# Where a ring slot is filled: normalised rows out of slot 7, half a matrix ahead of the ring

## The reference

```python
x = x + merged @ w_out[i]
hn = _rmsnorm(x, ffn_norm_g[i])
# _hier_moe: a group by softmax(hn @ wg), two experts in it by their logits
#   expert e: a = silu(xb @ w_gate[e]) * (xb @ w_up[e]);  y = a @ w_down[e]
x = x + _hier_moe(hn, ...)
return _rmsnorm(x, final_norm_g)
```

## Time and profile before

| | us |
|---|---|
| median of 3 runs (2300.44 to 2302.30) | 2300.65 |
| profiled execution, its own time | 2298.54 |
| its span | 2296.7 |
| TensorE busy | 2176.2 (95%) |
| TensorE weight loads (beside the matmuls) | 1131.4 (49%) |
| VectorE busy | 936.3 (41%) |
| ScalarE busy | 349.3 (15%) |
| GpSimd busy | 297.2 (13%) |
| bytes moved | 563.57 MB, 245 GB/s on average |

### The profile page before, as it was taken

The page is one execution under the profiler, slowest core; times in us unless marked ns, Lnnn a source line. Parts: engine busy times, 40 slices in busy tenths (PEclk is TensorE's granted clock), DMA queues, the critical chain, the costliest instruction groups (busy, mean ns, idle before and its releaser), DMA issues.

```text
span 2296.7 us, 23080 instructions
## 1 busy us (share of the span) xinstructions
PE 2176.2 (95%) x9050; PEld 1131.4 (49%) x9050; DVE 936.3 (41%) x1815; ACT 349.3 (15%) x678; POOL 297.2 (13%) x260
## 2 busy tenths in 40 slices
PE   9999999999999999999999999999999899888886
PEld 6544444475887644477588553333333333333332
DVE  2256544542876587537544342222222222222224
ACT  2015324201222200021101210000000000000001
POOL 0001121221376100001053010000000000000001
PEclk9999999999999999999999999999999999999999
DMA  7211110330333444483332499999999999999997
GB/s 291 101 56 47 55 46 10 115 151 10 110 131 132 160 183 183 172 149 116 128 138 110 201 345 425 427 426 426 426 427 427 426 427 426 426 427 427 427 427 278
DMA packets 75709, 563.57 MB, mean 245 GB/s; under 512 B 21202, under 2 KB 25938, under 8 KB 43152
## 3 DMA queue, kind: packets, MB, share of 16 engines
q1 hardware_dynamic: 52544, 530.70, 57.7%
q10 hardware_dynamic: 15136, 22.71, 3.0%
q0 software_dynamic: 7920, 8.67, 1.1%
HBM read 558.59 MB, written 27.82 MB: 255 GB/s over the span
## 4 chain that ended last, share of the span: by engine, by line
PE 69%; DMA 21%; DVE 6%; SPq 1%; issue 1%; ACT 1%; POOL 0%; DVEq 0%; ACTq 0%; POOLq 0%
DMA sb<-in_eu 13%; PE ps L1193 9%; PE ps L522 9%; PE ps L850 8%; DMA sb<-in_ed 8%; PE ps L429 7%; PE ps L1230 6%; PE ps L771 5%; PE ps L1006 5%; PE ps L454 3%; PE ps L1034 2%; PE ps L732 2%; DVE sb L1704 2%; PE ps L710 2%; PE ps L1164 2%; SPq L3064 1%
## 5 line engine op out<-in xcount | busy, mean ns | idle before, releaser
L1193 PE MATMUL ps<-sb 128*64 128x512 f32 x2048 | 463.0, 607 | 50.9 <-DMA sb<-in_eu 42.4
L1193 PEld LDWEIGHTS ps<-sb 128*64 128x64 f32 x2048 | 163.8, 139 | 337.1 <-issue 337.1
L1704 DVE TENSOR_TENSOR sb<-sb 128x1024 f32<-128x1024 f32 (+9 forms) x419 | 226.4, 573 | 86.3 <-PE ps L850 38.3
L522 PE MATMUL ps<-sb 128*128 128x512 f32 x512 | 236.7, 600 | 0.0
L1230 PE MATMUL ps<-sb 128*64 128x512 f32 x992 | 221.4, 599 | 14.0 <-ACT sb L1672 8.3
L850 PE MATMUL ps<-sb 128*128 128x512 f32 x448 | 193.4, 593 | 1.4 <-DVE sb L2255 1.4
L429 PE MATMUL ps<-sb 128*128 128x512 f32 (+1 forms) x464 | 188.9, 566 | 1.0 <-issue 1.0
L771 PE MATMUL ps<-sb 128*128 128x256 f32 x784 | 175.7, 383 | 3.6 <-DVE sb L2175 3.6
L771 PEld LDWEIGHTS ps<-sb 128*128 128x128 f32 x784 | 148.5, 191 | 25.3 <-DVE sb L2175 4.0
L1230 PEld LDWEIGHTS ps<-sb 128*64 128x64 f32 x992 | 70.6, 137 | 151.9 <-issue 134.9
L522 PEld LDWEIGHTS ps<-sb 128*128 128x128 f32 x512 | 91.0, 190 | 100.3 <-issue 98.6
(11 more groups left out here) (347 smaller groups left out, 2055.5 us busy)
## 6 DMA issues: line engine op xcount, KB each, us to landing
sb<-in_eu SPq DMA_DIRECT2D x63, 2048.0 KB, 36.7
sb<-in_eg SPq DMA_DIRECT2D x62, 2048.0 KB, 37.3
sb<-in_ed SPq DMA_DIRECT2D x60, 2048.0 KB, 37.3
sb<-in_m SPq DMA_DIRECT2D x16, 2048.0 KB, 7.4
sb<-in_m SPq DMA_DIRECT2D x16, 1024.0 KB, 4.9
sb<-in_mg SPq DMA_DIRECT2D x8, 1536.0 KB, 6.5
sb<-in_wo SPq DMA_DIRECT2D x4, 2048.0 KB, 7.7
sb<-in_winF SPq DMA_DIRECT2D x12, 512.0 KB, 3.5
```

Of the source, the lines that this page charges most:

```text
L522: ins = pe.matmul(o, lhsT, rhs, start=k == 0, stop=k == 7)
L1193: ins = pe.matmul(o[64 * e:64 * e + 64, :], x[:, k, 64 * e:64 * e + 64], weight(2 * mat + e)[:, 512 * k:512 * k + 512], start=k == 0, stop ...
L1704: return own(dve.tensor_tensor(o, a, b, op))
```

## The change

- `RING` has place 7 as its seventh entry in place of the tenth: matrix 6 goes there, once the mixer's last products are done; 7, 8 and 9 go to places 3, 1 and 5.
- The normalised rows of blocks 0 to 2 are staged, one after the other, in one buffer of 1024 columns in the constants that are done with, those of block 3 in `YE`. ScalarE waits for the row transfer before it reuses or goes on.
- `first_rows` reads the residual X in its place, with a step of 8 elements, and the one-hots carry the factor `block_r` of the norm.
- Matrix 10: its first half (2048 columns) goes to `FIRST_HALF`, also in the constants, once three row transfers have landed and the ranks and counts are done; the second half goes to its ring slot as before. Users get a column with the matrix, to find the half.
- The count matmuls stand ahead of the last rows of pair 0, `count_rounds` ahead of `weights`.
- The constants are ordered anew and padded by 40 columns.

```diff
-SBUF = 55940
-RING = (6, 2, 0, 4, 8, 9, 3, 1, 5, 7)
+SBUF = 55980
+RING = (6, 2, 0, 4, 8, 9, 7, 3, 1, 5)
+AHEAD = len(RING)
...
+        done_ck = SB[:, 4096 + CK_COLS["c01"][0]:4096 + CK_N + SM_N + 8 * 72 + 72 + 400]
+        at_ck = CK_COLS["neg"][0] - CK_COLS["c01"][0]
+        HELD = [view(done_ck, at_ck, 1024)] * 3 + [YE]
+        FIRST_HALF = view(done_ck, 0, 2048)
...
-                pe.wait_ge(S("hn_rows"), i + 1)
                 pe.wait_ge(S("first"), i + 1)
-                zr = Z[:, i, :].rearrange("p (b a) -> p b a", b=8)
+                zr = X[:, i, :].rearrange("p (a b) -> p b a", b=8)
...
             rank(3)
+            open_tile(pe, ("cnt",), 4)
+            for j in range(4):
+                ins = pe.matmul(T.ap("cnt")[:, 0:64], ck("ones"), ES[:, j, :], start=j == 0, stop=j == 3)
+            ins.then_inc(T.f("cnt"), 1)
             first_rows(2, 1)
...
+            def expert(n, at_):
+                return (FIRST_HALF if n == AHEAD and at_ < 2048 else slot("ex", n))[:, at_:at_ + 512]
...
-                act.activation(Z[:, i, :].rearrange("p (b a) -> p b a", b=8), X[:, i, :].rearrange("p (a b) -> p b a", b=8),
+                if i:
+                    act.wait_ge(S("hn"), 16 * i)
+                act.activation(HELD[i].rearrange("p (b a) -> p b a", b=8), X[:, i, :].rearrange("p (a b) -> p b a", b=8),
                                ACT.Copy, scale=block_r[:, i:i + 1]).then_inc(S("hn_rows"), 1)
                 act.wait_ge(S("hn_rows"), i + 1)
-                act.dma_start(hn_d[128 * i:128 * i + 128, :], Z[:, i, :]).then_inc(S("hn"), 16)
+                act.dma_start(hn_d[128 * i:128 * i + 128, :], HELD[i]).then_inc(S("hn"), 16)
...
                 for c in range(2):
-                    t = tt(OC[:, c, :], AM[:, c, i, :], bc(BM0[:, c, i], 1, 128), ALU.mult)
+                    t = own(dve.scalar_tensor_tensor(OC[:, c, :], AM[:, c, i, :], block_r[:, i:i + 1], bc(BM0[:, c, i], 1, 128),
+                                                     ALU.mult, ALU.mult))
...
             def weights():
+                count_rounds()
...
                     for e in range(2):
+                        if n + e == AHEAD and part < 2:
+                            continue
...
-                if n == 8:
+                if n == 6:
+                    sp.wait_ge(*T.full("mgp", 3, 3, 3))
+                if n == 9:
                     sp.wait_ge(*T.full("wo2", 3, 1))
-                if n == 9:
-                    sp.wait_ge(S("hn"), 64)
-                    sp.wait_ge(*T.full("xt", 0, 1))
+                if n == AHEAD:
+                    sp.wait_ge(S("hn"), 48)
+                    sp.wait_ge(*T.full("rank", 3))
+                    sp.wait_ge(*T.full("cnt"))
+                    for part in range(2):
+                        cols = slice(1024 * part, 1024 * part + 1024)
+                        sp.dma_start(FIRST_HALF[:, cols], EW[k // 2][2 * q + k % 2][:, cols]).then_inc(loaded("ex", n)[0], 16)
```

More of the change, by code:

```diff
@@ L40 @@
 CK_COLS = {}
-CK_N = _cols(CK_COLS, [("ident", 128), ("iota", 128), ("tok", 8), ("gf", 8), ("gx", 8), ("neg", 128), ("cneg", 124), ("c01", 124),
-                       ("tri", 128), ("ones", 128), ("cs", 256)])
+CK_N = _cols(CK_COLS, [("ident", 128), ("iota", 128), ("tok", 8), ("gf", 8), ("gx", 8), ("c01", 124), ("tri", 128), ("ones", 128),
+                       ("neg", 128), ("cneg", 124), ("cs", 256), ("pad", 40)])
 def bc(ap, axis, n):
@@ L362, in program @@
                                                                             H.rearrange("p a b -> p (a b)"), view(zone, 24576, 4096)]
-        done_ck = SB[:, 4096 + CK_COLS["neg"][0]:4096 + CK_N + SM_N + 8 * 72 + 72 + 400]
+        done_ck = SB[:, 4096 + CK_COLS["c01"][0]:4096 + CK_N + SM_N + 8 * 72 + 72 + 400]
+        at_ck = CK_COLS["neg"][0] - CK_COLS["c01"][0]
+        HELD = [view(done_ck, at_ck, 1024)] * 3 + [YE]
+        FIRST_HALF = view(done_ck, 0, 2048)
         OH = [view(zone, 4096 + 512 * n, 4, 128) for n in range(2)]
@@ L1130, in tensor_program @@
             ring[0] = 2
+            def expert(n, at_):
+                return (FIRST_HALF if n == AHEAD and at_ < 2048 else slot("ex", n))[:, at_:at_ + 512]
             for q in range(PAIRS):
-                pe_pair(pe, T, q, lambda n: loaded("ex", 6 * q + n), lambda n: slot("ex", 6 * q + n), any_bank, ("gather", q % 2, 16 * ((q + 1) // 2)))
+                pe_pair(pe, T, q, lambda n: loaded("ex", 6 * q + n), lambda n, at_: expert(6 * q + n, at_), any_bank, ("gather", q % 2, 16 * ((q + 1) // 2)))
                 if q == 0:
@@ L1140, in tensor_program @@
                     ins.then_inc(T.f("wtab"), 1)
[L1141 to L1144, removed]
                 for n in range(6):
@@ L1193, in pe_pair @@
                         ins = pe.matmul(o[64 * e:64 * e + 64, :], x[:, k, 64 * e:64 * e + 64],
-                                        weight(2 * mat + e)[:, 512 * k:512 * k + 512], start=k == 0, stop=k == 7)
+                                        weight(2 * mat + e, 512 * k), start=k == 0, stop=k == 7)
                     if table is T and q == 0 and k in (1, 3, 5):
@@ L1217, in pe_pair @@
                             d = 1024 * k + 512 * nh
-                            ins = pe.matmul(both[nh][64 * e:64 * e + 64, :], aT[:, k, 64 * e:64 * e + 64], weight(4 + e)[:, d:d + 512],
+                            ins = pe.matmul(both[nh][64 * e:64 * e + 64, :], aT[:, k, 64 * e:64 * e + 64], weight(4 + e, d),
                                             start=k == 0, stop=k == 3)
@@ L1229, in pe_pair @@
                         d = 1024 * k + 512 * nh
-                        ins = pe.matmul(o[64 * e:64 * e + 64, :], aT[:, k, 64 * e:64 * e + 64], weight(4 + e)[:, d:d + 512],
+                        ins = pe.matmul(o[64 * e:64 * e + 64, :], aT[:, k, 64 * e:64 * e + 64], weight(4 + e, d),
                                         start=k == 0, stop=k == 3)
@@ L1686, in results_taken @@
                 eng.wait_ge(*table.full("sp", q - 1, 3, 1))
+            elif table is T:
+                eng.wait_ge(S("hn"), 64)
         def act_end(act):
@@ L2557, in vector_program, with count_rounds @@
             dve_table(dve, own, T)
+            def count_rounds():
+                dve.wait_ge(*T.full("cnt"))
+                dve.tensor_reduce(cnt, T.ap("cnt")[:, 0:64], op=ALU.max, axis=AX.X).then_inc(T.s("cnt"), 1)
+                dve.wait_ge(*T.free("cnt"))
+                after(ts(cnt, cnt, float(CAP - 1), None, ALU.add))
+                after(own(dve.tensor_copy(NR, cnt)))
+                dve.tensor_scalar(NR, NR, CAP.bit_length() - 1, None, ALU.logical_shift_right).then_inc(S("rounds"), 1)
             def weights():
+                count_rounds()
                 for i in range(4):
@@ L2580, in weights @@
                 dve_rows(dve, own, ENDS, EVEN)
[L2583 to L2589, removed]
             for q in range(ENDS):
@@ L2594, in vector_program @@
                     copy(("wtab",), WTAB, T.ap("wtab")[:, 0:PAIRS])
-                    count_rounds()
                     after(own(dve.tensor_copy(TOKF, TAB)))
@@ L3096, in bank @@
                 return banks[0] - 1
-            pe_pair(pe, R_pair, 0, lambda n: (S(f"w{n}"), 16), lambda n: SLOT[n], bank, ("rgather", 0, 16))
+            pe_pair(pe, R_pair, 0, lambda n: (S(f"w{n}"), 16), lambda n, at_: SLOT[n][:, at_:at_ + 512], bank, ("rgather", 0, 16))
         def act_more(act):
```

## The result

| | us |
|---|---|
| before, median of 12 runs (2299.31 to 2302.30) | 2300.62 |
| changed, median of 12 runs (2300.28 to 2306.41) | 2305.35 |
| ratio | 1.0017, 95% interval [1.0010, 1.0025] |
| changed, again in a later set of 11 runs, before beside it 2299.96 | 2303.19, 1.0015 [1.0006, 1.0024] |
| profiled execution of the changed kernel, its span | 2303.5 |

The forecast was no measurable change (2300.1, range 2292.8 to 2302.6). The kernel is slower by about 4 us (3.9 by the ratio, 4.7 by the two medians), and its median lies above the range.

The account below looks back on a forecast made before the run. It took the saturated stream of expert matrices to bound the end: 7.4 us gained less (8.1 + 0.2 - 1.4) lost leaves 0.5 off 2300.65, so 2300.1 us, range 2292.8 to 2302.6.

Parts of the forecast that it names:

- old empty stretch: DMA nearly idle at 1292 to 1321 us, 19 GB/s; the early matrix was to land there by about 1297 us.
- The price of the step: Extra time of first_rows' TensorE loads reading X with a 32-byte step; priced from ScalarE and VectorE rows, 237 ns per load.
- d: Extra time per first_rows load and matmul record from the step, taken as 0.126 us, forecast range 0.08 to 0.14.
- D: Delay of TensorE's reaching pair 0, 64 records times the extra time of each; taken as 8.1 us.
- Slack: 1.4 us: Queue runs dry at 1368.7 us, next matrices give bytes at 1367.3; pair 0 may be that much late free of cost.
- Later supplies have 2 us in hand or more: Matrices refilled from 1378.0 us on were to arrive with at least 2 us before the queue runs dry.
- 7.4 us: Full gain from taking 1.5 matrices, 3.15 MB, out of the saturated stream at 427 GB/s.
- the sign of the slack: A pause of bytes just ahead of the issue answering to 1366.3 us, when pair 0 gives back its down matrices.
- my own formula: Gain of the whole kernel as 7.4 - max(0, D - 1.4) us, D being pair 0's delay.
- rival 4: Stream not at 427 GB/s after the address shift, or slot 7 not free in time; 2296 to 2306 us, chance 0.02.
- Rival 3: Loads before pair 0 take three times as long or more; 2307.9 us at d = 0.25, chance 0.07.
- Rival 1: Loads with the step cost nothing or little in first_rows, whole gain comes; 2293.3 us, chance 0.29.

Follow-up runs that it names:

- e1: Changed kernel, but first_rows reads 128 columns of X in one run instead of with a step of 8 elements; 2295.96 us, ratio 0.9984.
- e4: Changed kernel, but first_rows reads with a step of 4 elements in its first half, 2 in its second; one execution, loads 326 and 198 ns.
- e5: Changed kernel with rows staged in one run each in four borrowed places, matrix 6 three quarters early; 2294.88 us, ratio 0.9981.
- e3: Changed kernel without the half matrix held apart, the eleventh matrix loaded in quarters as before; 2303.35 us, ratio 1.0015.
- e9: Staged kernel e5 with 44 columns of padding instead of 40 and without the half matrix held apart; 2295.91 us, ratio 0.9983.
- e11: The changed kernel itself run again, nothing edited, beside the kernel before at 2299.96 us; 2303.19 us, ratio 1.0015.
- e7: Staged kernel e5 with 44 columns of padding instead of 40, so slots start at multiples of 64 bytes; 2293.54 us, ratio 0.9973.
- e6: Kernel before with only 40 columns of padding behind the constants, buffers behind them 160 bytes higher; 2301.39 us, ratio 1.0007.
- e8: Staged kernel e5 without the half matrix held apart; 2296.49 us, ratio 0.9986.
- e2: Kernel before with first_rows reading X with the step of 8 elements and one-hots carrying the norm's factor; 2303.80 us, ratio 1.0016.
- e10: e9 with the count matmuls and count_rounds moved back behind pair 0; 2295.55 us, ratio 0.9981.

## Why the prediction was wrong

**What held.** The stream bounds the end; matrix 6 lands in the old empty stretch; ten matrices and a half are issued before pair 0 (the prediction's sum has 10.5, its last paragraph says nine and a half). The price of the step held too: I took d = 0.126 us per record and D = 8.1 to 8.3. With the last load's own length taken off, the 23 steps of 24 loads went from (2.76 - 0.19) / 23 = 0.112 us to (5.83 - 0.34) / 23 = 0.239, d = 0.127, and the five groups of first_rows matmuls together from 8.1 to 16.2 us. The eight count records ahead of the last rows add 0.9 us and TensorE's old wait of 0.9 us for VectorE is gone; in e1 the two cancel (91.8 against 91.7). D was 7.8. ScalarE's and VectorE's rows were the right guide, and TensorE pays what they pay: 239 / 128 = 1.87 ns per column, where I took 1.85.

The reading of the earlier trace rows was wrong even so: L1204's load with a step of 16 bytes looked free because I set it beside ordinary loads of 192 ns. Transposes load faster in one run (141 to 146 ns), and 206 is a penalty. e4 shows it for ordinary loads: 326 ns. The rule cited from the Trainium skill (SBUF — State Buffer, Door 1: The DMA port swizzle), free up to 4 fp32 elements, doesn't hold for these loads; the page gives no price for a longer step either, so the price that I took came from the earlier trace rows alone. Nor does the count of columns alone in the Trainium skill (TensorE: Matmul & The Clock Gate, LDWEIGHTS (loading the stationary operand)). A step of 2 elements is nearly free, 4 isn't.

**The step that failed** is "Slack: 1.4 us", with the full queue under it, and with it "Later supplies have 2 us in hand or more". By the sum, D + 0.2 - 1.4 = 6.9 of the 7.4 us were to be lost. In the trace without the clock fall 7.4 + 2.8 = 10.2 were. From e1 to the changed kernel, one edit apart, pair 0 is 7.7 us later and the ratio rises by 0.31 to 0.33%, 7.1 to 7.6 us: the delay is paid in full, nothing of it is covered. Three things in the step were off.
- What the queue holds. The sum has 3.5 matrices lying in it from 1347.4 us on. But matrices 10 to 13 go to places that pair 0 itself gives back, quarter by quarter, and all but the half wait for it. In e1 SP issues the first quarter at 1347.16 and the second at 1348.88, one of matrix 11 each, since that part of matrix 10 has gone ahead: 0.52 MB in 1.72 us, or 305 GB/s, and the stream goes at 238 to 305 until two quarters come at a time. When pair 0 is late by D, its first quarter is too. That is why the empty stretch of the changed kernel stands at 1351 to 1356 us, ahead of the first quarter (issued at 1354.64), and not ahead of the down matrices, the place that I had named as the sign of the slack.
- The gathers. I gave each 128 rows, 0.52 MB. In the changed kernel their queue moves this between 1356 and 1363 us, in both first gathers together:

```profile
q0 software_dynamic: 288, 0.28, 11.8%
```

  Of the 288 packets 67 have 4096 bytes and the others 4, so slots without a token move next to nothing. That is 0.28 MB and not 1.05; 0.77 MB at 0.393 is 2.0 us of work that wasn't in the queue, and slack 1.4 turns into -0.6. I had also placed them behind the rows' last transfer. GpSimd's first gather in the changed kernel waits for VectorE's table, which comes with pair 0, so they didn't fill the empty stretch from 1351 us either:

```profile
1354.38 1.20 POOL L2888 DMA_INDIRECT sb<-hn_d,sb  x1 [14.09 <-DVE sb L2656]
```
- Later supplies. e1 has no delay (pair 0 at 91.8) and still gets 5.8 instead of 7.4. Of the missing 1.6 us, 1.1 are lost by 1358 us, in the thin stretch, and most of the rest between 1368 and 1372, where the down matrices' places are filled again (its bytes laid beside those of before, stretch by stretch). In e5 about 1 us more goes around the next supply: 359, 322 and 352 GB/s in the three stretches of 2 us from 1376 us on. It had no 2 us in hand.

Put into my own formula, e1's 1.6 us are a slack of -1.6 instead of 1.4. The sum then gives 7.4 - 7.8 - 1.6 = -2.0, against 2.8 slower in the trace: within the 0.8 of such a comparison.

**The rest of the difference** is the drift, 1.0 us: the shift by 160 bytes, which I had counted as nothing and given a chance of 0.02 with the rest of rival 4. 2.8 + 1.0 = 3.8 us; the ratio of 1.0017 is 3.9.

**Rivals.** Rival 3, slower, was right in sign and wrong in its cause: it set the point from which nothing is left at d = 0.138. With a slack of -1.6 that point is D = 5.8, d = 0.09, and the step alone, at the price I forecast, lies beyond it. Rival 1 described e1 and e5, not this kernel; its full 7.4 us never came. The chance of 0.08 for slower hung on a slack that stood on one estimate of bytes and had no range of its own. It should have had one of 3 us to either side.

**The clock.** In the first trace of the changed kernel the granted clock was 0.5 in 1370 to 1372 us (1.2 GHz in place of 2.4), behind 14 us of expert matmuls at 1.00 and two short waits; it made the 32 down records 8.78 us instead of 7.09. This isn't tied to the change: the same fall is in e3, e4 and e9, and not in e11, e1, e5 or e7. Falls ahead of the ring also make whole traces start apart. The one trace without any, e9, issues its first expert matrix at 1249.0 us, the three with one fall at 1249.4 to 1250.8, the four with two at 1251.1 to 1252.2, and the five with three (one of them twice as long counted as two) at 1252.5 to 1253.4.

## What to carry to other kernels

When a stream is the bound, a free place earlier is worth its bytes only as long as something is left to issue when the queue runs dry. Work out that point with the real bytes of every transfer in it, ask of each whether it can be issued yet or waits for the very work that is late, and give the point a range. An engine whose waits look like slack may have covered for another: in the old order 3.4 us of a row transfer hid half of the same delay. An operand read with a step in fp32 should be priced by a probe of that engine at that step: staging the rows in one run in four borrowed places turned a loss of 0.17% into a gain of 0.19%. With the slots at multiples of 64 bytes it was 0.27%; by their intervals the two aren't told apart, by the drift in the traces they are.

## What the runs showed of the hardware

- Weight loads of 128 x 128 in fp32 against the step in bytes: 4: 192 ns, 8: 198, 16: 326, 32: 337. Their pace in a row: 0.112 us in one run (before), 0.239 us with 32 bytes (changed).
- Where all slots start 48 bytes past a multiple of 64, the stream of 16 KB rows lost 1.0 to 1.3 us in 800 us (some 0.15%) against the kernel before, whose slots start 16 bytes past one, in eight of eight traces (changed twice, e1, e3, e4, e5, e6, e8). 16 bytes past it or at it, the four others (e2, e7, e9, e10) differ from it by at most 0.2 us. The cause inside the memory wasn't looked for.
- A scalar_tensor_tensor of 128 x 128 in SBUF took 0.62 us for two where two tensor_tensor took 0.49: my nothing from the earlier trace rows was 0.07 each. In the changed kernel first_rows shows no wait for VectorE.
